# Two-layer hybrid decoder trunk on one core: the first two heads' high and low parts made ahead of the attention stage, one selection round moved into mixer B, nine convolution taps on GpSimd instead of seven

## The reference

```python
h = x @ w_in
qa, ka, va, qi, ki, wi, cq, ckv, kr, conv_in, gate_pre = jnp.split(h, IN_SPLITS, axis=-1)
y_a = dsa_attention(rope(qa), rope(ka), va, rope(qi), rope(ki), wi)    # 8 heads, top-128 keys per query
qb = rms_norm(cq, q_norm_g) @ w_uq      # 8 heads of 64 + 32 (rotary) columns
kvb = rms_norm(ckv, kv_norm_g) @ w_ukv  # 8 heads of 64 (key) + 64 (value)
y_b = causal_attention([q_nope, rope(q_rope)], [k_nope, rope(kr)], v_b)
y_c = silu(layer_norm(depthwise_conv31(a * sigmoid(g)) + conv_b))      # 512 channels
merged = sum(sigmoid(gate_pre_i + b_gate_i) * (y_i @ w_branch[i]) for the three)
x = layer_norm(ALPHA * x + merged @ w_out)
x = layer_norm(ALPHA * x + silu-gated ffn(x) + sigmoid(x @ Wg) * (p @ Wp))
```

## Time and profile before

| | |
|---|---|
| median of 3 runs | 1787.94 us |
| profiled execution, its own time | 1791.97 us |
| span of the profiled core | 1790.2 us |
| TensorE busy in the span | 1754.8 us |
| VectorE, ScalarE, GpSimd busy | 1282.3, 967.9, 814.7 us |
| mean granted TensorE clock | 0.992 |
| attention stage, layer 0 | about 165 to 367 us |
| attention stage, layer 1 | about 1052 to 1254 us |

### The profile page before, as it was taken

The page is one execution under the profiler, slowest core; times in us unless marked ns, Lnnn a source line. Parts: engine busy times, 40 slices in busy tenths (PEclk is TensorE's granted clock), DMA queues, the critical chain, the costliest instruction groups (busy, mean ns, idle before and its releaser), DMA issues.

```text
span 1790.2 us, 29252 instructions
## 1 busy us (share of the span) xinstructions
PE 1754.8 (98%) x10142; PEld 1540.3 (86%) x10142; DVE 1282.3 (72%) x2489; ACT 967.9 (54%) x1909; POOL 814.7 (46%) x464
## 2 busy tenths in 40 slices
PE   9999999999999999999999989999999999999997
PEld 9877788878789999988898878888787899999886
DVE  6279889967798888813363888898777988887033
ACT  4544787844476565622244548777444665555222
POOL 5445762354433334354434557624444334334542
PEclk9999999999999999999999999999999999999999
DMA  5333221123332333233333332221233332322331
GB/s 191 97 94 114 71 85 60 60 71 94 103 116 100 106 108 97 93 118 106 95 99 103 96 104 70 77 67 61 72 106 96 105 117 96 119 95 95 115 99 68
DMA packets 50410, 171.92 MB, mean 96 GB/s; under 512 B 6240, under 2 KB 6496, under 8 KB 50272
## 3 DMA queue, kind: packets, MB, share of 16 engines
q1 hardware_dynamic: 49408, 168.84, 30.0%
q10 hardware_dynamic: 864, 1.28, 0.2%
HBM read 162.76 MB, written 2.10 MB: 92 GB/s over the span
## 4 chain that ended last, share of the span: by engine, by line
PE 61%; DVE 5%; issue 2%; ACT 2%; POOL 2%; DMA 0%; DVEq 0%; SPq 0%; ACTq 0%; POOLq 0%
PE banks L1223 18%; PE banks L1225 18%; PE banks L1224 18%; PE banks L1280 1%; PE banks L1282 1%; PE banks L1281 1%; PE banks L1395 1%; PE banks L1345 1%; POOL sb_wl L661 1%; DVE sb_u L1942 0%; DVE sb_work L1724 0%; DVE sb_xl L1949 0%; DVE sb_u L1912 0%; PE banks L1451 0%; ACT sb_wh L807 0%
## 5 line engine op out<-in xcount | busy, mean ns | idle before, releaser
L661 POOL TENSOR_TENSOR sb_wl<-sb_wraw,sb_wh 128x1024 fp32r<-128x1024 f32 x205 | 501.3, 2449 | 611.7 <-ACT sb_wh L807 585.8
L1223 PE MATMUL banks<-sb_xh,sb_wh 128*128 128x512 f32 (+1 forms) x1152 | 406.3, 353 | 1.8 <-ACT sb_h_qa L983 0.8
L1225 PE MATMUL banks<-sb_xh,sb_wl 128*128 128x512 f32 (+1 forms) x1152 | 391.2, 340 | 0.0
L1224 PE MATMUL banks<-sb_xl,sb_wh 128*128 128x512 f32 (+1 forms) x1152 | 390.4, 339 | 0.0
L807 ACT ACTIVATE sb_wh<-sb_wraw 128x1024 fp32r<-128x1024 f32 x199 | 210.2, 1057 | 258.2 <-PE banks L1225 152.7
L1225 PEld LDWEIGHTS banks<-sb_xh,sb_wl 128*128 128x128 f32 x1152 | 220.2, 191 | 24.7
L1223 PEld LDWEIGHTS banks<-sb_xh,sb_wh 128*128 128x128 f32 x1152 | 221.1, 192 | 22.9 <-issue 3.3
L1224 PEld LDWEIGHTS banks<-sb_xl,sb_wh 128*128 128x128 f32 x1152 | 221.2, 192 | 14.2
L1223 PE MATMUL banks<-sb_t_hi,sb_wh 128*128 128x256 f32 x768 | 218.3, 284 | 3.6 <-DVE banks L2214 3.6
L1225 PE MATMUL banks<-sb_t_hi,sb_wl 128*128 128x256 f32 x768 | 218.3, 284 | 0.0
L1224 PE MATMUL banks<-sb_t_lo,sb_wh 128*128 128x256 f32 x768 | 218.1, 284 | 0.0
(11 more groups left out here) (357 smaller groups left out, 4007.9 us busy)
## 6 DMA issues: line engine op xcount, KB each, us to landing
sb_wraw<-in_weights SPq DMA_DIRECT2D x256, 512.0 KB, 3.5
sb_wraw2a<-in_weights SPq DMA_DIRECT2D x24, 512.0 KB, 3.7
sb_wraw2b<-in_weights SPq DMA_DIRECT2D x24, 512.0 KB, 4.5
sb_u<-in_x SPq DMA_DIRECT2D x8, 256.0 KB, 6.4
sb_q_raw<-sb_qn_t SPq DMA_DIRECT2D x16, 128.0 KB, 2.3
sb_k_raw<-sb_kn_t SPq DMA_DIRECT2D x16, 128.0 KB, 2.3
out<-sb_u SPq DMA_DIRECT2D x8, 256.0 KB, 2.1
sb_praw<-in_ple ACTq DMA_DIRECT2D x2, 512.0 KB, 4.1
```

What stands on the lines that cost most here:

```text
L661: nc.gpsimd.tensor_tensor(wl[:, t % WS, :], wraw[:, t % 2, :], wh[:, t % WS, :].bitcast(F32), ALU.subtract).then_inc(lo_ready, 1)
L1223: nc.tensor.matmul(out, wh_, xh_, start=start, stop=False, skip_group_check=onto)
L1224: nc.tensor.matmul(out, wh_, xl_, start=False, stop=False, skip_group_check=onto)
L1225: return nc.tensor.matmul(out, wl_, xh_, start=False, stop=stop, skip_group_check=onto)
```

## The change

- The rotary keys' four transposes join the eight of the rotary queries, in a step `ropes` at the same place in the front stage; ScalarE copies the key highs there, VectorE subtracts their lows after nine selection rounds (`key_low`). The rotation of the queries comes after five rounds instead of seven.
- The highs of heads 0 and 1 are copied by ScalarE at the end of the front stage (`heads`). Their lows, and the value low of head 0, go to GpSimd; VectorE's `lows` of head 0 disappear.
- On GpSimd the head lows of a tile now come ahead of its taps. Taps 0 and 1 follow the low of g3, taps 2 and 3 that of g4, then one each up to g9: nine in all, two fewer on VectorE.
- The front stage has 10 selection rounds and the last of the front (the 11th) stands at the start of the attention stage; the five others are dealt over slots 2 to 16. Slots 15 and 16 have one VectorE tap instead of two.

```diff
-PREP = {4 * h - 3: ("B", h) for h in range(1, BH)}
+PREP = {4 * h - 3: ("B", h) for h in range(2, BH)}
-SELECT_ROUNDS, SELECT_FRONT = TOPK // 8, 12
+SELECT_ROUNDS, SELECT_FRONT = TOPK // 8, 11
-POOL_TAPS = 7
-POOL_TAPS_AT = {T_GATE + LEAD + n: range(n, n + 1) for n in range(POOL_TAPS)}
-HEAD_LOW_AT = {T_GATE + LEAD + n: h for h, n in enumerate((1, 2, 4, 5, 6, 8, 9), 1)}
-V_LOW_AT = {T_GATE + LEAD + n: h for h, n in enumerate((2, 3, 5, 6, 7, 9, 10), 1)}
+POOL_TAPS = 9
+POOL_TAPS_AT = {T_GATE + LEAD + n: range(2 * n, 2 * n + 2) if n < 2 else range(n + 2, n + 3) for n in range(POOL_TAPS - 2)}
+HEAD_LOW_AT = {T_GATE + LEAD + n: (h,) for h, n in enumerate((2, 4, 5, 6, 8, 9), 2)}
+HEAD_LOW_AT[T_GATE + 2] = (0, 1)
+V_LOW_AT = {T_GATE + LEAD + n: h for h, n in enumerate((0, 2, 3, 5, 6, 7, 9, 10))}
-    steps = [("rope", 0), ("prep", ("B", 0)), ("prep keys", ("B", 0))]
-    steps += [("part", p) for p in parts[:DK]]
+    steps = [("part", p) for p in parts[:DK]]
-FRONT += [("tile", t) for t in range(T_U, T_GATE - 2)] + [("rope queries", 0)]
-FRONT += [("tile", t) for t in range(T_GATE - 2, T_GATE)]
+FRONT += [("tile", t) for t in range(T_U, T_GATE - 2)] + [("ropes", 0)]
+FRONT += [("tile", t) for t in range(T_GATE - 2, T_GATE)] + [("heads", 0)]
...
                 for t in range(T_GATE, T_OUT):
                     low(t, first)
-                    for k in POOL_TAPS_AT.get(t, ()):
-                        tap(layer, k)
-                    if t in HEAD_LOW_AT:
-                        h = HEAD_LOW_AT[t]
+                    for h in HEAD_LOW_AT.get(t, ()):
                         pool.wait_ge(b_high, layer * 2 * BH + (2 * h + 2))
...
+                    for k in POOL_TAPS_AT.get(t, ()):
+                        tap(layer, k)
...
+                    if kind == "ropes":
+                        act.wait_ge(ropes_turned, layer + 1)
                         for c in range(2):
                             nc.scalar.activation(qr_t[:, c], psum[:, 2 + c, :], ACT.Copy).then_inc(qr_out, 1)
+                        act.wait_ge(scored, layer * 12 + 12)
+                        for c in range(2):
+                            nc.scalar.activation(k_h[BN:BQ, c, :], psum[BN:BQ, 4, :], ACT.Copy).then_inc(rope_high, 1)
+                        continue
+                    if kind == "heads":
+                        for h in range(2):
+                            head_queries(layer, h)
+                            head_keys(layer, h)
+                        for h in range(2):
+                            head_values(layer, h)
                         continue
...
-            def turn_rope_queries(layer):
+            def turn_ropes(layer):
                 pe.wait_ge(roped_u, layer * 2 + 2)
-                pe.wait_ge(group_out, layer * OUTS + (OUTS - NT))
+                pe.wait_ge(group_out, layer * OUTS + OUTS)
...
+                for b in range(NT):
+                    last = nc.tensor.transpose(psum[0:BQ, 4, b * P:b * P + P], small[:, 64 + b * BR:64 + b * BR + BQ],
+                                               ident[:])
...
                 pe.wait_ge(qr_out, layer * 2 + 2)
+                pe.wait_ge(key_low, layer + 1)
...
-                    if n == 6 * 7 - 1:
+                    if n == 6 * 5 - 1:
                         dve.wait_ge(group_out, layer * OUTS + (OUTS - 3 * NT))
                         x = uqr[:].rearrange("p t (h d) -> p t h d", h=BH)
                         rope(x, BH, BR // 2, AD // 2, x, roped_u, layer * 2 + 2)
                     if n == 6 * 8 - 1:
                         conv_input(2)
+                    if n == 6 * 9 - 1:
+                        dve.wait_ge(rope_high, layer * 2 + 2)
+                        for c in range(2):
+                            ins = v.tensor_tensor(k_l[BN:BQ, c, :], psum[BN:BQ, 4, :], k_h[BN:BQ, c, :].bitcast(F32),
+                                                  ALU.subtract)
+                        ins.then_inc(key_low, 1)
```

More of the change, by code:

```diff
@@ L144 @@
 for _slot in range(UNITS):
-    _n = 1 if _slot <= KEEP_SLOT and (_slot not in PREP or PREP[_slot][0] != "B") else 2
+    _n = 1 if _slot <= KEEP_SLOT and _slot % 4 != 1 else 2
     TAPS_AT.append(TAPS[_taps:_taps + _n])
@@ L191 @@
 for _kind, _n in STEPS:
-    if _kind in ("rope", "turn", "value") or _kind == "prep" and _n[0] == "A":
+    if _kind in ("turn", "value") or _kind == "prep" and _n[0] == "A":
         _item = (_kind, _n)
@@ L817, in arrived @@
                     act.wait_ge(turned, turns + (TURN_AT[(kind, n)] + 1))
[L819 to L823, removed]
-                def prepare(which):
[L826 to L837, removed]
-                    n = which[1]
[L839 to L842, removed]
+                def prepare(which):
+                    n = which[1]
+                    act.wait_ge(score_ready, units + (last_reader(which) + 1))
+                    arrived("prep", which)
+                    bank = BANK_AT[("prep", which)]
+                    nc.scalar.activation(q_h[0:AD, n % 2, :], psum[0:AD, bank, :], ACT.Copy)
+                    nc.scalar.activation(q_l[AD:P, n % 2, :], psum[AD:P, bank, :], ACT.Copy).then_inc(turn_out, 1)
                 def exponentials(n):
@@ L880, in attention @@
                         gate(T_GATE + n[0], first, 6 + n[0] % 2, gate_at(g, j), column("bg", g * DK + j), gate_done)
-                    elif kind == "rope":
-                        rope_keys()
+                    elif kind == "prep" and n[0] == "A":
+                        prepare(n)
                     elif kind == "prep":
-                        prepare(n)
+                        head_queries(layer, n[1])
                     elif kind == "prep keys":
-                        prepare_keys(n)
+                        head_keys(layer, n[1])
+                        head_values(layer, n[1])
                     elif kind == "turn":
@@ L1359, in score @@
                     if qt == 0:
[L1360 to L1364 removed]
+                        if hd < BH:
+                            pe.wait_ge(b_low, (layer * BH + hd + 1) * 2)
                         else:
@@ L1383, in value @@
                     if hd < BH:
-                        if hd == 0:
-                            pe.wait_ge(v_first, layer + 1)
-                        else:
-                            pe.wait_ge(v_low, layer * (BH - 1) + hd)
+                        pe.wait_ge(v_low, layer * BH + (hd + 1))
                     else:
@@ L1411, in attention @@
                             last.then_inc(tile_used, 1)
-                    elif kind == "rope":
-                        turn_blocks("rope", 0, [small[:, 64 + b * BR:64 + b * BR + BQ] for b in range(NT)], BQ)
                     elif kind == "prep" and n[0] == "A":
@@ L1497, in _ @@
                         scratch(n, layer)
-                    elif kind == "rope queries":
-                        turn_rope_queries(layer)
+                    elif kind == "ropes":
+                        turn_ropes(layer)
+                    elif kind == "heads":
+                        continue
                     elif n in tile_group:
@@ L1817, in attention, with lows @@
-                lows("rope", 0)
-                lows("prep", ("B", 0))
-                lows("prep keys", ("B", 0))
+                def lows(which):
+                    n, bank = which[1], BANK_AT[("prep", which)]
+                    dve.wait_ge(turn_out, turns + (TURN_AT[("prep", which)] + 1))
+                    v.tensor_tensor(q_h[AD:P, n % 2, :], psum[0:AD, bank, :], q_h[0:AD, n % 2, :].bitcast(F32),
+                                    ALU.subtract)
+                    v.tensor_tensor(q_l[0:AD, n % 2, :], psum[AD:P, bank, :], q_l[AD:P, n % 2, :].bitcast(F32),
+                                    ALU.subtract).then_inc(qk_low, 1)
@@ L1836, in attention @@
                     if slot in PREP and PREP[slot][0] == "A":
-                        lows("prep", PREP[slot])
+                        lows(PREP[slot])
                     if TURN_LAG <= slot < UNITS + TURN_LAG:
```

54 lines of the change are left out of this document (16 added, 38 removed).

## The result

The changed kernel takes 1791.97 us (median of 9 runs, 1789.88 to 1793.71); the kernel before, beside it, 1787.43 us (1785.16 to 1788.77). The ratio is 1.0024, interval 1.0015 to 1.0032: slower by 0.24%, 4.5 us. The forecast was 1794.0. The profiled execution took 1793.71 us, with a span of 1791.8 and a mean granted clock of 0.992.

A forecast was written before the change was run, and what follows sets the result against it. TensorE, busy for 98% of the span, bounds the kernel. With 19.5 us gone and 25.6 new (13.6 pauses, 12.0 clock), net 6.1 slower: 1794.0 us for the median; own range 1787 to 1800, with rivals 1768 to 1801.

The forecast's parts named there:

- The chain: Layer 1, slot 5's score to head 1's value matmuls, through GpSimd's lows, head 3's read, ScalarE's copy: 19.9 us, before 17.3.
- TensorE's own way: Layer 1, TensorE's own time from slot 5 to head 1's value matmuls: 16.3 to 16.4 us, leaving a 3.5 us pause.
- The signs named as right: No key-low or rotary-transpose waits; ScalarE idle 3 us or more; pauses of about 3.5 and 3.3 us; clock under 1.
- those named as wrong: Weight low of g6 before slot 9's score, clock staying 1.00, or TensorE waiting for masks or value lows.
- (1) to (4): TensorE losses removed: rotated queries 2.8, first mask 1.0, key lows 8.4, clock 6.1; with value-matmul waits 1.2, 19.5 us.
- term 4: Head 3's first score: the tap no longer stands ahead of the head lows; 1.1 us gained.
- the term of 6.1: Low clock behind the 3.6 us pause at head 1 in each layer, going with it: 3.2 + 2.9 us.
- Rival D: Front stage: early rotation brings nothing, value copy-out or `key_low` wait replaces it; 2.8 us less gain, 1797 us, chance 0.05.
- The early rotation: Front stage: queries rotated two selection rounds earlier, removing TensorE's wait of 1.40 us; gain 2.8 us.
- The order on GpSimd: Tap behind the wait at g5 and g9 delays weight lows 2.9 us: pauses of 13.6 us, clock 12.0 us.
- the 4.0 us of the profiled execution: Profiled execution before lay 4.0 us above the runs; carried over: 1798.1 for such an execution, 1794.0 for the median.
- VectorE's 1.8 us a layer: Slots 2 to 16: one more round less two taps on VectorE; taken as nothing, other bound 1.8 us a layer.

The follow-up runs named there:

- e4: The kernel before with only the head lows of a tile put ahead of its tap on GpSimd: 1795.90 us, ratio 1.0047.
- e1: The changed kernel with GpSimd's taps put ahead of the head lows of their tile: 1779.44 us, ratio 0.9950.
- e3: The changed kernel with head 3's read behind the load of g7 instead of g8, head 6's behind g11 instead of g12: 1772.55 us, ratio 0.9912.
- e12: The changed kernel with taps ahead of head lows, seven GpSimd taps and the extra selection round back ahead of mixer B: 1771.59 us, ratio 0.9919.
- e11: e3 with the queries rotated after seven selection rounds of the front stage, as before: 1778.23 us, ratio 0.9940.
- e6: The changed kernel with the 12th selection round put back ahead of mixer B: 1786.74 us, ratio 0.9994.
- e8: The changed kernel with seven GpSimd taps, ahead of the head lows; as e12 but with the round dealt in: 1776.60 us, ratio 0.9939.
- e5: The changed kernel with the edits of e1 and e3, taps first and both reads earlier: 1770.68 us, ratio 0.9903.
- e13: The changed kernel with the edits of e1, e3 and e6, taps first, reads earlier and round back: 1771.42 us, ratio 0.9914.

## Why the prediction was right, and by which steps

**Direction and size held: 1794.0 forecast, 1791.97 measured.** The chain was as drawn: the weight low behind the wait, SyncE's read behind that, ScalarE's copy, the lows of probabilities, the value matmuls of heads 1 and 4. In layer 1 it can be checked term by term, from slot 5's score at 1064.87: 4.3 to the head lows, 6.1 to the weight low, 2.4 for that, 0.4 to the read, 4.9 to ScalarE's copy, 1.9 to the value matmul, 20.0 us where 19.9 were forecast. TensorE's own way there took 16.3, as forecast, and the pause 3.69 against 3.5. The signs named as right are there (no wait for key lows or at the rotary transposes, ScalarE idle 2.90 and 4.52 us for the reads where 3 or more was named, all four pauses, the clock under 1), and none of those named as wrong. e4 shows the order alone making these pauses, e1 shows them shorter, e3 gone.

**(1) to (4), what goes.** 19.5 us forecast, 2.8 us of them outside the stage. e12, which has only this part and the old order, keeps head 3's wait of 1.1 (term 4), and 1.6 us of waits at head 1's value are left, so 16.8 should have gone; measured 14.5. The profiles agree better: 1790.2 - 1769.8 = 20.4, of which 3.4 are the two falls outside the stage, 17.0. The difference is the clock again. No run shows the term of 6.1 (3.2 and 2.9) as a time. What the one profiled execution shows is 6.83 and 6.82 us at a clock of 0.50, 12.2 of them behind the pauses of 3.63 and 3.64 us, and TensorE busy for 389.5 us in the two stages, against 382.6 in e12; a typical run of the kernel before had less low clock to give back. Rival D is out in its `key_low` form: no such wait appears. The early rotation is worth at least the 2.8 us (e11).

**The order on GpSimd.** Pauses of 13.6 us forecast, 16.1 measured; clock 12.0 (4 x 3.0, an estimate) against 11 by half of the time at 0.50, an estimate too, or 9.5 by the busy time. So 25.6 became 26 to 27, and the stage grew by 7.9 us where the sum gives 16.7 gone and 25.6 new, 8.9.

**A step that did not hold, and luck in the total.** The forecast carried the 4.0 us of the profiled execution over and put the changed kernel's own at 1798.1. That execution took 1793.71, 1.7 us above the profiled one of before and not 6.1. The median lies 4.5 above the median of before, because the clock of the typical run of before is higher (0.995) than in its profile (0.992), and that of the changed kernel is not. The two falls outside the stage are in no term of the sum. That 6.1 for profiled executions stands so near to 4.5 for medians is in part luck.

**The step that was mis-sized** is VectorE's 1.8 us a layer, taken as nothing. Its bound was "1.8 us a layer"; by e6 the round costs 5.4 us in all, 2.7 a layer: 1.9 us more of pause at head 4, and, in the one profile of each kernel, a clock that falls at 4.46 and 4.14 us but not at 2.61 and 2.23. (The 1.8 us were the round less two taps; e6 moves the round of 3.3 alone.) The cover named for it, slots that start earlier, is no cover where VectorE is a link in the chain to ScalarE's key copy. This raised head 4's pauses to 4.46 and 4.14 against 3.3; without it they are 2.61 and 2.23, so there the order had been priced too high by about 0.9 us. The two errors cancelled in part.

**The tap as the whole delay.** The forecast took GpSimd's wait of 4.67 us at g5 for given, and a tap behind it as the whole loss. At g5 the wait was only 0.91 us, since GpSimd's added work, 5.8 us of taps above all, had filled it (5.66 with seven taps). For head 3, order and load both delay the read, which is why e1 alone did not reach e3. For head 6 the wait was 4.78 us and the order counts. It did not show in the forecast, because the wait still ends with ScalarE's key copy, 4.3 us behind slot 5's score where 4.5 were forecast, whether GpSimd stood idle until then or worked.

**How the parts add up**, in ratios: the early split 0.9919; with the round 0.9939; with nine taps 0.9950; with the head lows ahead of the taps 1.0024. In us of 1787: 14.5 won, then 3.6, 2.0 and 13.2 lost. Only the last step is clear of the intervals; the 3.6 and the 2.0 have pauses in the traces to show for them, but no interval of their own. A part worth 14.5 us stood beside an order of a few lines that cost nearly as much.

**The reads, and what they took.** The two reads moved by one tile gave 20 us (e3). In the changed kernel the 64 KB read that ScalarE waits for at head 3 took 4.4 us from issue to use, from 1078.61 to 1083.01, right behind the load of a 512 KB tile, issued at 1077.70. The median from issue to landing of all 16 such reads is 2.1 us in that profile, so this place takes longer than most; that the tile's load ahead makes it so is likely and not shown.

## What to carry to other kernels

Work may be free inside a wait and cost its length behind it: in the kernel before, the tap of 2.9 us stood ahead of GpSimd's wait of 4.67 us, and the value matmuls of heads 1 and 4 waited 0.44 and 0.41 us; with it behind that wait, nothing else changed, four pauses of 2.98 to 3.46 us came (e4). So when instructions are reordered, look at who is queued behind the engine's next release, not at the engine's busy share. A transfer that was late by 0.20 us is the thing to move first: once the two reads stood one tile earlier, the order on GpSimd and the extra round made no difference that these runs can tell (seven taps with early reads were not run). And a VectorE step dealt into a slot was not hidden here where VectorE had no time left in it (busy for 2.09 of 2.09 us ahead of a pause of 1.40 us, e8), nor where another engine's copy, on which a read depends, comes after it (head 4's pauses are 1.9 us shorter without the round, e6). Last, look at the clock of the profiled execution against those of the other runs before a term for it goes into a sum.

## What the hardware showed that was not expected

The clock fell in portions. In windows of 0.5 us, which read 0.50 at the lower level, each stretch at the lower level at an attention pause is 3.4 or 6.8 us long, and the same kernel shows both (3.4 with the pause of 3.69 us; 6.8 with those of 3.83, 4.14 and 4.46 us). Nearly equal pauses differ: 3.46 us has 6.8 and 3.44 us has 3.4 (e4). Which pauses brought it about was not a matter of length alone: 2.50 and 2.88 us did (e1), 2.61 and 2.23 did not (e6), and the pause of 1.7 to 1.9 us at the same matmul outside the stage did at both places (534 and 1421) in the kernel before, at one of them in e1, e5, e6, e11 and e13, and at neither in the changed kernel and the other seven. In e11 the clock also fell at 883 us, for 3.4 us, with no pause over 0.2 us ahead of it. Here, by the estimate of half of the time at 0.50, a pause may cost its length alone or 1.7 to 3.4 us more, so a forecast of a few pauses has at least that spread.
